# An encoder layer on one core: the first projections in shorter spans, with the input tiles turned inside them

## The reference

```
xn   = rmsnorm(x, norm1_g)
proj = xn @ w_in                       # pooling | q | k | v | output gate | 16 mLSTM gates
a    = multiscale_pool(proj[pooling], pool_w, pool_scale)      # windows 2, 4, 8, 16
m    = bidir_mlstm(proj, gate_b, head_norm_g)                  # 4 heads, chunks of 128
x    = x + concat(a, m) @ w_out
x    = x + hier_moe(rmsnorm(x, norm2_g), router, experts)      # 2 of 32 experts a token
y    = rmsnorm(x, final_norm_g)
```

## Time and profile before

| | |
|---|---|
| median of 3 runs | 1279.34 us (1278.87 to 1282.72) |
| the profiled execution | 1283.91 us, its span 1282.2 us |
| busy: PE, DVE, ACT, POOL | 1159.6, 876.6, 687.0, 185.2 us |
| PE busy, in 0 to 8 / 8 to 20 / 20 to 23 / 23 to 28 us | 0.00 / 7.86 / 0.07 / 5.00 us |
| PE busy, in 31 to 54 / 54 to 88 / 88 to 120 us | 22.64 of 23 / 32.81 of 34 / 30.39 of 32 us |
| granted clock of PE, mean over the span | 0.957 |

### The profile page before, as it was taken

The page is one execution under the profiler, slowest core; times in us unless marked ns, Lnnn a source line. Parts: engine busy times, 40 slices in busy tenths (PEclk is TensorE's granted clock), DMA queues, the critical chain, the costliest instruction groups (busy, mean ns, idle before and its releaser), DMA issues.

```text
span 1282.2 us, 18679 instructions
## 1 busy us (share of the span) xinstructions
PE 1159.6 (90%) x6071; PEld 980.2 (76%) x6071; DVE 876.6 (68%) x1410; ACT 687.0 (54%) x1122; POOL 185.2 (14%) x260
## 2 busy tenths in 40 slices
PE   5999999999999979999299999999999999999920
PEld 4887888888799968887178788888888888888810
DVE  4639510110188845665579999999999999999958
ACT  4431231221165653233277877787778777877733
POOL 1100200000010211212202211221122212211100
PEclk9999989999999989999599999999999999999965
DMA  8212230210011054552779999999999999999757
GB/s 228 56 33 74 97 109 1 66 33 33 1 50 51 2 165 134 162 181 98 261 239 359 369 382 384 378 373 389 388 383 381 390 382 385 375 383 383 276 225 303
DMA packets 119699, 287.30 MB, mean 224 GB/s; under 512 B 22448, under 2 KB 53680, under 8 KB 119648
## 3 DMA queue, kind: packets, MB, share of 16 engines
q1 hardware_dynamic: 103744, 245.02, 52.5%
q0 software_dynamic: 15904, 41.61, 8.9%
HBM read 261.76 MB, written 37.92 MB: 234 GB/s over the span
## 4 chain that ended last, share of the span: by engine, by line
PE 50%; DVE 7%; ACT 3%; DMA 2%; issue 2%; POOL 0%; ACTq 0%; SPq 0%; POOLq 0%; DVEq 0%
PE psum L643 15%; PE psum L645 14%; PE psum L644 14%; DVE e_lo L1543 3%; ACT e_hi L1113 3%; PE psum L857 2%; PE psum L815 1%; PE psum L890 1%; DVE x L1660 1%; DVE x L1668 1%; DVE x L1658 1%; PE psum L803 1%; DMA gx<-xn_scratch,rows_to 1%; DMA f_y<-expert_rows 0%; PE psum L782 0%
## 5 line engine op out<-in xcount | busy, mean ns | idle before, releaser
L1543 DVE TENSOR_TENSOR e_lo<-e_st,e_hi 128x1024 fp32r<-128x1024 f32 x384 | 442.5, 1217 | 16.9 <-ACT e_hi L1113 15.8
L1113 ACT ACTIVATE e_hi<-e_st 128x1024 fp32r<-128x1024 f32 x384 | 372.3, 1050 | 10.4 <-PE psum L645 9.5
L643 PE MATMUL psum<-e_hi,ex_hi 128*128 128x512 f32 x512 | 204.5, 399 | 8.9 <-DVE ex_lo L1591 3.7
L644 PE MATMUL psum<-e_lo,ex_hi 128*128 128x512 f32 x512 | 200.9, 392 | 0.0
L645 PE MATMUL psum<-e_hi,ex_lo 128*128 128x512 f32 x512 | 200.7, 392 | 0.0
L643 PE MATMUL psum<-xT_hi,w_hi 128*128 128x512 f32 (+1 forms) x408 | 147.5, 362 | 6.9 <-DVE w_lo L1227 3.8
L644 PE MATMUL psum<-xT_lo,w_hi 128*128 128x512 f32 (+1 forms) x408 | 146.3, 359 | 0.0
L645 PE MATMUL psum<-xT_hi,w_lo 128*128 128x512 f32 (+1 forms) x408 | 146.0, 358 | 0.0
L643 PEld LDWEIGHTS psum<-e_hi,ex_hi 128*128 128x128 f32 x512 | 96.7, 189 | 41.8 <-DVE e_lo L1543 16.5
L645 PEld LDWEIGHTS psum<-e_hi,ex_lo 128*128 128x128 f32 x512 | 96.8, 189 | 21.0
L644 PEld LDWEIGHTS psum<-e_lo,ex_hi 128*128 128x128 f32 x512 | 96.9, 189 | 19.1
(11 more groups left out here) (233 smaller groups left out, 1876.5 us busy)
## 6 DMA issues: line engine op xcount, KB each, us to landing
e_st<-in_expert_w_gate_dram SPq DMA_DIRECT2D x128, 512.0 KB, 5.8
e_st<-in_expert_w_up_dram SPq DMA_DIRECT2D x128, 512.0 KB, 6.4
e_st<-in_expert_w_down_dram SPq DMA_DIRECT2D x128, 512.0 KB, 8.5
w_st<-in_w_in_dram SPq DMA_DIRECT2D x20, 512.0 KB, 4.2
xn_scratch<-xn POOLq DMA_DIRECT2D x20, 512.0 KB, 3.8
f_y<-expert_rows SPq DMA_DIRECT2D x20, 512.0 KB, 12.3
out_dram<-x SPq DMA_DIRECT2D x10, 512.0 KB, 4.8
x_in<-in_x_sample_dram POOLq DMA_DIRECT2D x8, 512.0 KB, 5.5
```

What stands on the lines that cost most here:

```text
L643: pe.matmul(out, a_hi, b_hi, start=start, stop=False)
L644: pe.matmul(out, a_hi, b_lo, start=False, stop=False)
L1113: act.activation(e_hi[:, r, :, :], e_st[:, slot, :, :], ACT.Copy).then_inc(ehi_done, 1)
L1543: dve.tensor_tensor(e_lo[:, r, :, :], e_st[:, slot, :, :], e_hi[:, r, :, :].bitcast(F32), ALU.subtract).then_inc(elo_done, 1)
```

## The change

It touches the head alone:

- A second table of spans, `SPANS`, adds tokens 0 to 255 and 256 to 511. The three u slices on tokens 0 to 511 become six groups: three on the first 256 tokens, then three on the next 256 (groups 0 to 5; the gates are groups 6 to 8 now, and all later numbers move up by three).
- PE starts group 0 after two tiles. Tile 2 is turned inside group 0 and tile 3 inside group 1, each after the first half of the k loop; tile 4 after group 2, 5 after 3, 6 after 4, 7 after 5, 8 and 9 after 6.
- PE issues 19 matmuls of `ident` with itself into PSUM bank 3, which nothing reads (`keep_warm`): 8 before tile 0 is turned, 3 before tile 1, 8 before group 0.
- ACT and DVE split weight slice 0 ahead of tile 0's parts, slice 1 between tiles 2 and 3, slice 2 before tile 3's parts, slice 3 after tile 4's.
- SP waits for tile 1's load before it issues slice 1. POOL issues tile 2's load after it has made `ident`, not before.

```diff
--- before.py
+++ after.py
@@ -41,6 +41,7 @@
     NL = GR + E
     CAP = T
     SEGS = [(0, 512), (512, 512), (1024, 256)]
+    SPANS = SEGS + [(0, 256), (256, 256)]
     assert (NT, KD, NG, H, KF, E) == (10, 8, 4, 4, 4, 32) and D == 1024
 
 
@@ -286,7 +287,7 @@
 
         proj, mixer_after = [], {}
         NS = len(SEGS)
-        proj += [("u", U + c, 0) for c in range(NG - 1)]
+        proj += [("u", U + c, NS + half) for half in range(2) for c in range(NG - 1)]
         proj += [("g", G, s) for s in range(NS)]
         proj += [("u", U + c, s) for s in range(1, NS) for c in range(NG - 1)]
         for first, count, kind in ((U_LAST, 1, "u"), (O, H, "o"), (K, H, "k"), (Q, H, "q")):
@@ -295,6 +296,7 @@
                 if kind == "o" and s > 0:
                     mixer_after[len(proj) - count] = (2 * s - 2, 2 * s - 1)
         NPROJ = len(proj)
+        N_FIRST = 2 * (NG - 1)
 
         last_use = {m: n + 1 for n, (_, m, _) in enumerate(proj)}
         parts_after = {}
@@ -406,6 +408,7 @@
             sp.dma_start(x_in[:, 0, :], tokens(0, x_prompt, x_sample)).then_inc(first_load, 16)
             sp.dma_start(g1_b[:, :], norm1_g[0:1, :].broadcast_to([P, D])).then_inc(g1_in, 16)
             slice_in(0)
+            sp.wait_ge(x_load[1], 16)
             slice_in(1)
             for dst, src in (
                 (wpool[:, :, :], pool_w[0].rearrange("g c e -> c g e")),
@@ -513,14 +516,13 @@
                     pool.wait_ge(xn_done, t - 2)
                 pool.dma_start(x_in[:, t % 3, :], tokens(t, x_prompt, x_sample)).then_inc(x_load[t % 3], 16)
 
-            for t in range(1, 3):
-                x_in_tile(t)
+            x_in_tile(1)
             pool.memset(gbias[:, :], 0.0).then_inc(bias_zero, 1)
             pool.memset(ident[:, :], 0.0).then_inc(pool_step, 1)
             pool.wait_ge(pool_step, 1)
             pool.affine_select(out=ident[:, :], in_=ident[:, :], compare_op=ALU.not_equal, fill=1.0, base=0,
                                pattern=[[-1, P]], channel_multiplier=1).then_inc(consts_done, 1)
-            for t in range(3, NT):
+            for t in range(2, NT):
                 x_in_tile(t)
                 if t == 5:
                     pool.wait_ge(wlo_done, G - 1)
@@ -662,9 +664,19 @@
                 last.then_inc(xt_ready, 1)
 
             pe.wait_ge(consts_done, 1)
-            for t in range(4):
-                x_transposes(t)
-            transposed_after = {0: (4,), 1: (5, 6), 2: (7, 8), 3: (9,)}
+
+            def keep_warm(count):
+
+                for _ in range(count):
+                    pe.matmul(psum[:, 3, 0:P], ident[:, :], ident[:, :], start=True, stop=True)
+
+            keep_warm(8)
+            x_transposes(0)
+            keep_warm(3)
+            x_transposes(1)
+            keep_warm(8)
+            transposed_inside = {0: 2, 1: 3}
+            transposed_after = {2: (4,), 3: (5,), 4: (6,), 5: (7,), 6: (8, 9)}
 
             def mix_pooled(g):
                 if g == 0:
@@ -685,13 +697,15 @@
 
 
             for n, (kind, m, s) in enumerate(proj):
-                a, length = SEGS[s]
+                a, length = SPANS[s]
                 pe.wait_ge(wlo_done, m + 1)
                 pe.wait_ge(xlo_done, (a + length) // P)
                 bank_free(pe, n)
                 for k in range(KD):
                     last = product3(psum[:, n % 4, 0:length], (w_hi[:, m % 4, k, :], w_lo[:, m % 4, k, :]),
                                     (xT_hi[:, k, a:a + length], xT_lo[:, k, a:a + length]), k == 0, k == KD - 1)
+                    if n in transposed_inside and k == KD // 2 - 1:
+                        x_transposes(transposed_inside[n])
                 last.then_inc(proj_ready, 1)
                 for t in transposed_after.get(n, ()):
                     x_transposes(t)
@@ -941,15 +955,17 @@
             def take(n):
 
                 kind, m, s = proj[n]
-                a, length = SEGS[s]
+                a, length = SPANS[s]
                 src = psum[:, n % 4, 0:length]
                 if kind != "g":
                     act.wait_ge(proj_ready, n + 1)
                 if kind == "u":
                     g = min(m, NG - 1)
                     act.wait_ge(pads_zero, 1)
-                    parts = [(0, pos[0], S0), (S0, pos[1], length - S0)] if s == 0 else [(0, pos[1] + a - S0, length)]
+                    parts = [(0, pos[0], S0), (S0, pos[1], length - S0)] if a == 0 else [(0, pos[1] + a - S0, length)]
                     for col, first, w in parts:
+                        if w == 0:
+                            continue
                         ins = act.activation(u_ext[:, g, first:first + w], src[:, col:col + w], ACT.Copy)
                     ins.then_inc(act_took, 1)
                 elif kind == "o":
@@ -984,7 +1000,8 @@
 
             act.activation(stat[:, 1, 0:1], epsc[:, :], ACT.Sqrt).then_inc(root_done, 1)
             act.wait_ge(root_done, 1)
-            for t in range(NT):
+
+            def x_root(t):
                 if t == 0:
                     act.wait_ge(first_load, 16)
                 else:
@@ -994,14 +1011,28 @@
                 act.wait_ge(sq_done, t + 1)
                 act.activation(stat[:, 1, t:t + 1], stat[:, 0, t:t + 1], ACT.Sqrt, bias=epsc[:, :],
                                scale=1.0 / D).then_inc(root_done, 1)
-                if t >= NT - 2:
-                    take(t - NT + 2)
-                if t >= 1:
-                    x_part(t - 1)
-                if 3 <= t < 7:
-                    w_part(t - 3)
-            x_part(NT - 1)
-            for n in range(2, NPROJ):
+
+            x_root(0)
+            x_root(1)
+            w_part(0)
+            x_part(0)
+            x_part(1)
+            x_root(2)
+            w_part(1)
+            x_root(3)
+            x_part(2)
+            w_part(2)
+            x_root(4)
+            x_part(3)
+            x_root(5)
+            for t in range(4, NT):
+                take(t - 4)
+                x_part(t)
+                if t == 4:
+                    w_part(3)
+                if t + 2 < NT:
+                    x_root(t + 2)
+            for n in range(N_FIRST, NPROJ):
                 take(n)
 
 
@@ -1244,18 +1275,33 @@
                 ins = dve.memset(u_ext[:, :, first:first + width], 0.0)
             ins.then_inc(pads_zero, 1)
             dve.wait_ge(g1_in, 16)
-            for t in range(NT):
+
+            def x_norm(t):
                 dve.wait_ge(root_done, t + 2)
                 link(dve.reciprocal(stat[:, 1, t:t + 1], stat[:, 1, t:t + 1]))
                 if t >= 2:
                     dve.wait_ge(xt_ready, t - 1)
                 dve.scalar_tensor_tensor(out=xn[:, t % 2, :], in0=x_in[:, t % 3, :], scalar=stat[:, 1, t:t + 1],
                                          in1=g1_b[:, :], op0=ALU.mult, op1=ALU.mult).then_inc(xn_done, 1)
-                if t >= 1:
-                    x_part(t - 1)
-                if 3 <= t < 7:
-                    w_part(t - 3)
-            x_part(NT - 1)
+
+            x_norm(0)
+            x_norm(1)
+            w_part(0)
+            x_part(0)
+            x_part(1)
+            x_norm(2)
+            w_part(1)
+            x_norm(3)
+            x_part(2)
+            w_part(2)
+            x_part(3)
+            x_norm(4)
+            for t in range(4, NT):
+                if t + 1 < NT:
+                    x_norm(t + 1)
+                x_part(t)
+                if t == 4:
+                    w_part(3)
 
             def pool_group(g):
```

## The result

The changed kernel takes 1283.74 us (median of 20 runs, 1279.48 to 1286.71). The kernel before, run beside it, takes 1281.36 us (median of 20, 1278.87 to 1284.36). The ratio is 1.0018, 95% interval 1.0010 to 1.0027: no difference by the 0.3% bound, and if anything slower. The forecast was 5.7 us faster. In another set of runs both were measured again: 1.0014 (0.9999 to 1.0029) for the changed kernel, 1.0002 (0.9991 to 1.0014) for the kernel before against itself.

What follows compares the result with a forecast made beforehand. PE was taken as the bound, short of normalised tiles early (12.4 us of waits) and starting at low clock. The first wide u group moves from 61.67 to 55.9: 5.8 us, less 0.1 for handovers; 1279.34 becomes 1273.6, range 1271.6 to 1278.0.

Steps and rivals of the forecast that it cites:

- Group 0 at 15.4: Head, PE: group 0 starts at 15.4, after tile 1 is normalised, 7.5 us earlier than before.
- The clock up at about 19: Head, PE: the clock rises at about 19, between bounds of 18.2 and 21.8.
- Unread products at 0.11 us each: Head, PE: unread products take 0.11 us each at the high level, about 0.22 at the low; all 19 cost nothing.
- Constants out at 17.6: SP's queue: pooling matrices issue in 0.5 us instead of 5.38, so the constants end at 17.6.
- Slice 2's landing in 4.8 us: Head, load of slice 2: 4.0 us alone plus 0.8 for tile 5's load, landing at 22.4.
- PE waits 0.8 us for tile 4, group 3 at 29.35: Head, PE: after group 2 it waits 0.8 us, turns tile 4 and starts group 3 at 29.35.
- From group 3 on, 26.5 us: PE, from group 3 through the gate groups: 26.5 us together, to the first wide u group at 55.9.
- All later stages hang on PE: After the head: PE or something it feeds releases every later stage, so the 5.7 us saved stay saved.
- Rival B: Head: slice 2 lands at 26.5; 1277.7 us, or about 1280.3 if PE's standing drops the clock; chance 0.08.
- A: Head: turned tiles cut PE's early products, so the clock rises late; 1275.5 to 1279.1 us; chance 0.10.
- C: Head: as A, but the clock stays low until the gates' group 6; slower, 1291.4 us; chance 0.05.
- D: Head: slice 2 lands at 21.1 and the clock is up by 18; gain 7.1, 1272.2 us; chance 0.09.

Runs made afterwards that it cites:

- experiment 3: Changed kernel with 20 more unread products ahead of group 2, filling PE's wait: 1281.82 us, ratio 1.0008.
- Experiment 7: Changed kernel with weight slices 2 and 3 both issued ahead of the constants on SP's queue: 1273.11 us, ratio 0.9941.
- experiment 8: Changed kernel with slices 2 and 3 issued ahead of the constants and without the 19 unread products: 1278.43 us, ratio 0.9986.
- experiment 9: Kernel before, with slices 2 and 3 issued ahead of the constants: 1283.30 us, ratio 1.0013.
- experiment 1: Changed kernel without SP's wait for tile 1 ahead of slice 1: 1277.48 us, ratio 0.9976.

## Why the prediction was wrong

The forecast was 1273.6 us in a range of 1271.6 to 1278.0, and measured were 1283.74. The step that failed is "So the constants end at 17.6, and slice 2 (4.0 us alone) lands at 22.4, with 0.8 added for tile 5's load": the constants ended at 19.40, slice 2 landed at 26.52, and PE waited 5.46 us for it where the prediction had 0.1. Point by point:

- **Group 0 at 15.4:** right (15.64). Tile 1, the split of slice 0 and the order on ACT and DVE came as worked out.
- **The clock up at about 19:** the direction was right, the size not. I counted from the unread products at 12.96, but it was up at about 6 in the first profile and 12 in the second. With tile 3 turned from 20.93, PE was ready for group 2 at 23.3, where I had 24.7. This made the gap longer, not the kernel faster.
- **Unread products at 0.11 us each:** half of what they are. Eight of them are x16 in the timeline and take 1.95 us at the high level, 0.24 each. I had read the x4 of a row as four whole products. They cost nothing all the same, since the last ends at 13.85, before group 0 is ready.
- **Constants out at 17.6:** 19.40. The step took the 5.38 us of the pooling matrices for a stall that would vanish, and it did (0.66), but the time came back at the constants behind them: 10.3 us for eleven, not 8.4. I had taken the stall for a property of one DMA, and it moved to whichever issue came next. That the queue is full then is my reading; no view shows how full it is.
- **Slice 2's landing in 4.8 us:** 7.1. I took the 4.0 us of a slice issued in a calm stretch instead of the nearer row, 8.9 us for slice 0 in the same crowded head. I had counted one tile's load beside it, and there were two; that they are the cause is not shown, as no run takes them away. The two errors, 1.8 and 2.3 us, make 4.1 of landing.
- **PE waits 0.8 us for tile 4, group 3 at 29.35:** 34.60. PE waited for slice 2 itself, 5.46 us, and the fall of the clock added about 1 (experiment 3).
- **From group 3 on, 26.5 us:** 27.0, right.
- **All later stages hang on PE:** right. Experiment 7's head is 6.5 and 7.9 us shorter than in the two profiles of the kernel before, and its time is 7.4 us shorter in the same runs.

Rival B has the course of what happened: slice 2 at 26.5, PE standing over 4 us, the clock dropping, a price of 1280.3, 1 us over the median I had, where 2.4 us over the kernel before were measured. It had a chance of 0.08. That its 26.5 is the measured number is luck: B has the pooling matrices stall for 5.38 us and the slice land in 4.0, and measured were 0.66 and 7.1, with 1.9 us more at the other constants. Rivals A and C are refuted by experiment 8, and D would have needed slice 2 at 21.1; experiment 7, where it lands by 19.0, takes 1273.1, near D's 1272.2.

In the head the changed kernel is no better than the kernel before, and 0 to 1.5 us worse. The medians differ by 2.4 us. Of the 1 to 2.4 us that are left, the estimate from all runs puts 1 to 2 us in low clock of the later stages. Median less head is 1219.7 and 1221.2 us for the kernel before, 1222.1 and 1221.6 for the changed one, and from 1218.7 to 1222.0 in the other nine, so kernels with the same stages behind the head scatter as much. Why the changed kernel should meet more low clock there, with the same work behind the head, stays open, and chance is not excluded: without a dip in the head experiments 8 and 9 still have 56.4 and 55.6 us of low clock, as much as the changed kernel has less its dip.

## What to carry to other kernels

When a change makes an engine want a load earlier, follow the queue that issues it, from the moment its buffer is free: here the head's 7 us hung on small loads that had been harmless for as long as the buffer came free after them. Bound a landing by loads of the same crowded stretch, not by the median of calm ones. Products that nobody reads are worth their place only if real work follows without a gap; put the work's inputs in order first.

## What the runs showed of the hardware

- **Small loads hold a queue for long.** The twelve constants, 426 KB in all by the sizes of their issues, keep SP busy for 11 us (8.43 to 19.40) in the changed kernel and for 8 us in experiment 7 (24.37 to 32.33), and the stall moves to another of them when one is relieved: 4.72 us at the pooling matrices in experiment 1, 0.66 in the changed kernel with 2.21 at the router's weights (11.64). The wait ahead of slice 1 cost 5.2 us of issue at its place (8.4 less 3.2) and still 2.3 at the end of the queue (19.44 against 17.14).
- **Unread products raise the clock, and idling takes it back.** In the kernel before it had risen with them by 8.0 and had fallen by group 0, at 22.3, after a stretch with 1.93 us of work in 7 (0.67). In the changed kernel it fell within 24 to 28, after PE had stopped at 23.3.
- **Products of 256 columns** are 0.12 us apart at the high level and 0.21 at the low, half of the 0.23 and 0.43 of 512 columns: the shorter spans cost PE almost nothing.
